# Layer 0's input tiles 0, 1, 6 to 9 by seven products, two modulation blocks behind the query heads, another order at the start, and a folded Fourier product

## The reference

```python
mx = jnp.split((silu_c @ w_mod[l] + b_mod[l])[:, None, :], N_MOD, axis=-1)
mc = jnp.split(silu_cc @ w_mod[l] + b_mod[l], N_MOD, axis=-1)
zx = modulate(rms_norm(x, norm1_g[l]), mx[0], mx[1]) @ w_in[l]
zc = modulate(rms_norm(ctx, norm1_g[l]), mc[0], mc[1]) @ w_in[l]
fx, cqx, ckvx, krx, gx = jnp.split(zx, SPLITS, axis=-1)
...
y = jnp.fft.fftn(u, axes=(1, 3), norm="ortho").real
...
u = a * jax.nn.sigmoid(g)
```

## Time and profile before

| | us |
|---|---|
| median of 3 runs | 1775.14 (1773.23 to 1775.78) |
| the profiled execution | 1775.64 |
| its span | 1772.7 |
| TensorE busy | 1712.4 (97%) |
| VectorE busy | 1013.2 (57%) |
| ScalarE busy | 415.1 (23%) |
| POOL busy | 315.2 (18%) |
| mean transfer rate | 145 GB/s over the span |

### The profile page before, as it was taken

One profiled execution on the slowest core, in us unless ns is written; L12 is line 12 of the kernel. 1 busy time (PEld: TensorE's weight loads), 2 busy tenths in 40 slices (PEclk: granted clock), 3 DMA queues, 4 the chain that ended last, 5 costly groups with the idle time before them and its releaser, 6 DMA issues.

```text
span 1772.7 us, 27384 instructions
## 1 busy us (share of the span) xinstructions
PE 1712.4 (97%) x11010; PEld 1388.0 (78%) x11010; DVE 1013.2 (57%) x1936; ACT 415.1 (23%) x806; POOL 315.2 (18%) x355
## 2 busy tenths in 40 slices
PE   7999999999999999999999999999999999999997
PEld 5434456688888888756799998877888787899997
DVE  1238666756676444496488764277831432288883
ACT  1312463322102110336322110323421101211110
POOL 0000271133001220006144110077000000001110
PEclk9999999999999999999999999999999999999999
DMA  7885324232233252321544555343222443344452
GB/s 274 321 315 197 132 106 170 80 135 95 98 140 115 76 190 91 123 96 34 228 167 167 170 168 187 119 141 129 89 74 86 154 144 118 119 146 164 167 172 91
DMA packets 38744, 256.32 MB, mean 145 GB/s; under 512 B 4161, under 2 KB 7361, under 8 KB 9057
## 3 DMA queue, kind: packets, MB, share of 16 engines
q1 hardware_dynamic: 34544, 228.29, 36.6%
q0 software_dynamic: 3504, 22.15, 3.2%
q10 hardware_dynamic: 576, 4.19, 0.6%
HBM read 247.28 MB, written 7.34 MB: 144 GB/s over the span
## 4 chain that ended last, share of the span: by engine, by line
PE 86%; DVE 8%; ACT 2%; DMA 1%; POOL 1%; issue 1%; ACTq 0%; SPq 0%; DVEq 0%; POOLq 0%
PE ps L707 85%; DMA ring<-weights 1%; POOL aux L2037 1%; PE ps L957 1%; DVE arena L2255 1%; DVE aux L2284 1%; DVE arena L2285 1%; DVE arena L2286 1%; DVE ring L2318 0%; DVE small L2297 0%; DVE aux L2186 0%; DVE aux L2187 0%; DVE aux L2191 0%; DVE aux L2190 0%; DVE aux L2188 0%
## 5 line engine op out<-in xcount | busy, mean ns | idle before, releaser
L707 PE MATMUL ps<-hT,ring 128*128 128x256 f32 (+3 forms) x2976 | 637.1, 374 | 6.8 <-DVE aux L2381 2.1
L707 PEld LDWEIGHTS ps<-hT,ring 128*128 128x128 f32 (+1 forms) x2976 | 505.2, 189 | 125.9 <-issue 64.2
L707 PE MATMUL ps<-arena,ring 128*128 128x256 f32 (+3 forms) x1884 | 355.5, 344 | 4.7 <-DVE arena L2286 3.4
L707 PEld LDWEIGHTS ps<-arena,ring 128*128 128x128 f32 (+1 forms) x1884 | 298.5, 191 | 50.9 <-issue 13.0
L707 PE MATMUL ps<-arena,sums 128*128 128x128 f32 (+1 forms) x966 | 161.6, 317 | 1.3 <-DVE aux L2373 1.3
L707 PEld LDWEIGHTS ps<-arena,sums 128*128 128x128 f32 x966 | 141.7, 191 | 12.3 <-DVE aux L2373 2.5
L2015 POOL TENSOR_TENSOR aux<-aux 128x256 f32<-128x256 f32 (+1 forms) x40 | 41.9, 1047 | 373.3 <-ACT aux L1566 304.4
L2317 DVE TENSOR_TENSOR sums<-ring 128x512 f32<-128x512 f32 x86 | 60.1, 699 | 64.1 <-PE ps L707 59.3
L707 PE MATMUL ps<-hT,sums 128*128 128x128 f32 (+1 forms) x616 | 95.1, 301 | 0.4 <-DVE aux L2373 0.4
L707 PEld LDWEIGHTS ps<-hT,sums 128*128 128x128 f32 x616 | 83.7, 191 | 5.3 <-DVE aux L2373 0.8
L2037 POOL TENSOR_SCALAR aux<-aux,small 128x512 f32<-128x512 f32 (+1 forms) x48 | 71.2, 1492 | 79.5 <-DVE small L2304 78.8
(11 more groups left out here) (384 smaller groups left out, 1980.2 us busy)
## 6 DMA issues: line engine op xcount, KB each, us to landing
ring<-weights SPq DMA_DIRECT2D x212, 1024.0 KB, 4.9
arena<-ahead POOLq DMA_DIRECT2D x8, 1024.0 KB, 9.4
kept_turns<-aux ACTq DMA_DIRECT2D x4, 1024.0 KB, 5.9
arena<-kept_turns POOLq DMA_DIRECT2D x6, 512.0 KB, 4.5
kept_keys_values<-spare POOLq DMA_DIRECT2D x1, 2048.0 KB, 8.4
hT<-ahead POOLq DMA_DIRECT2D x2, 1024.0 KB, 6.1
spare<-ahead POOLq DMA_DIRECT2D x2, 1024.0 KB, 12.3
arena<-kept_keys_values POOLq DMA_DIRECT2D x1, 2048.0 KB, 9.0
```

The source lines that it names most:

```text
L707: ins = nc.tensor.matmul(o_, lhsT, rhs, start=start, stop=stop, skip_group_check=True)
```

## The change

1. The pairs of tiles (6, 7), (8, 9), (0, 1) of layer 0 are computed as quads with seven products. The activations' forms lie where the query heads will be (`qT`). Blocks 4, 5 stand before the first pair, 6, 7 before the second, 8 before the third, 9 behind tile 4, 10 behind the query heads, 11 behind the values. VectorE's sums, forms and combinations are placed by hand; the third pair is combined after ten taps.
2. The turn, the read and the gain that belong to blocks 4 to 11 move into the attention, the turn into step 1, the read and the gain into step 2 (`MOD_BEHIND_TURN, MOD_BEHIND_READ = 1, 2`); the blocks of layer 1 move from steps 2, 5, 8, 11 to 4, 7, 10, 13.
3. The Fourier product over the tokens computes the cosine part for 129 and the sine part for 127 columns of each side; VectorE makes the other half by symmetry (`unfolded`).
4. At the start the memory's tiles are the first transfers of SyncE; ScalarE issues the tables, the vectors and the condition; the table of the root comes first, Silu later; keys 0 and 1 come before block 0; TensorE multiplies zeros five times before the memory's sums and six times behind them.

```diff
@@ constants
-MOD_TURN_STEP = 13
-MOD_READ_STEP = 15
-MOD_STEP = {2: 0, 5: 1, 8: 2, 11: 3}
+MOD_TURN_STEP = 15
+MOD_READ_STEP = 17
+MOD_STEP = {4: 0, 7: 1, 10: 2, 13: 3}
+TAPS_AHEAD = 10
+FOLD = T // 2 + 1
+FOLDED = ((0, FOLD), (1, FOLD - 1))
+STILL = (5, 6)
+Z_PAIRS = ((6, 7), (8, 9), (0, 1))
+MOD_BEHIND = (MOD_BLOCKS - 2, MOD_BLOCKS - 1)
+MOD_BEHIND_TURN, MOD_BEHIND_READ = 1, 2
@@ weight_stream
+    keys(0, 2)
     mod(0, 0)
-    keys(0, 2)
+    keys(2, 4)
     mod(0, 1)
-    keys(2, 6)
+    keys(4, 6)
     mod(0, 2)
...
+        if l == 0:
+            whole()
+            mod(0, 4)
+            mod(0, 5)
+            for p, pair in enumerate(Z_PAIRS):
+                for role in range(4):
+                    for j in range(4):
+                        out.append((("z", 0, 0, p, 0, role, j), "w_in", 0, z_tile(0, pair[role // 2], 2 * j + role % 2)))
+                for q in ((6, 7), (8,), ())[p]:
+                    mod(0, q)
...
+            if l == 0 and n == 4:
+                mod(0, 9)
@@ TensorE
-            pe.wait_ge(S["first_loaded"], 48)
+            def still(count):
+                for _ in range(count):
+                    nc.tensor.matmul(ps[:, 4, 0:T], zeros[:, 0:P], zeros, start=True, stop=True, skip_group_check=True)
+            pe.wait_ge(S["zeros"], 1)
+            still(STILL[0])
+            pe.wait_ge(S["first_loaded"], 16)
...
+            still(STILL[1])
+            mem_keys(0, 2)
             pe.wait_ge(S["silu_c"], 2)
             mod_block(0, 0)
-            mem_keys(0, 2)
+            mem_keys(2, 4)
...
+                def z_seven(p):
+                    n_quad = quad_first[0, 0, "z", p, 0]
+                    for i, (wf_, af) in enumerate(PRODUCTS):
...
+                        for j in range(4):
+                            if wf_ in ROLES:
+                                lhsT = weight(("z", 0, 0, p, 0, ROLES[wf_], j))
+                            else:
+                                lhsT = sums[:, n_quad % 2, SUMS[wf_], j * P:(j + 1) * P]
+                            if i == 2 and j == 0:
+                                pe.wait_ge(S["quad_sums"], n_quad + 1)
+                            mm(bank(key)[:, o:o + T], lhsT, z_act(af, j, p), o == 0 and j == 0, j == 3,
+                               key if (o + T == 512 or i == 6) and j == 3 else None)
+                if l == 0:
+                    mod_block(0, 4)
+                    mod_block(0, 5)
+                    z_seven(0)
+                    mod_block(0, 6)
+                    mod_block(0, 7)
+                    z_seven(1)
+                    mod_block(0, 8)
+                    z_seven(2)
                 for i, n in enumerate(Z_ORDER):
+                    if l == 0 and any(n in pair for pair in Z_PAIRS):
+                        continue
...
-                    if l == 0:
-                        q = MOD_FIRST + i
-                        if q < MOD_BLOCKS:
-                            mod_block(0, q)
-                        if q == MOD_BLOCKS:
-                            mod_turn(0, 1)
                     if n == 4:
+                        if l == 0:
+                            mod_block(0, 9)
                         kr_sum(l)
...
@@ behind the query heads, before the keys' nope part
+                if l == 0:
+                    mod_block(0, MOD_BEHIND[0])
...
@@ fy: cosines to 0:129 of each side, sines to 129:256, 16 products of 129 and 127 columns
-                            for part, tb in ((0, "cn"), (1, "sn")):
+                        for part, tb in ((0, "cn"), (1, "sn")):
+                            first, end = FOLDED[part] if l == 0 else (0, T)
+                            a = sd * T + (FOLD if l == 0 and part == 1 else 0)
+                            for j in range(2):
...
@@ ahead of fy(0)
+                    mod_block(0, MOD_BEHIND[1])
...
@@ in the attention's steps
+                    if l == 0 and j == MOD_BEHIND_TURN:
+                        mod_turn(0, 1)
@@ ScalarE
+            act.dma_start(tab[:, 0:NTAB_FIRST], table_in[:, 0:NTAB_FIRST]).then_inc(S["first_loaded"], 16)
+            act.dma_start(vec[:, :], vectors).then_inc(S["vec_loaded"], 16)
+            act.dma_start(cs_raw[:, :, :], c_in).then_inc(S["c_loaded"], 16)
+            act.wait_ge(S["zeros"], 1)
+            table_of(ACT.Sqrt, zeros[:, 0:1])
...
@@ squares of the memory and the root, and only then
+            did(f(cs[:, :, CS_WIDE - 32:CS_WIDE - 30], cs_raw[:, :, :], ACT.Silu), "silu_c", wait=False)
+            table_of(ACT.Sqrt)
...
+                if l == 0:
+                    for p, pair in enumerate(Z_PAIRS):
+                        first_product(0, "z", 0, p)
+                        taken(act, ("z", 0, 0, p, 3))
+                        for n in pair:
+                            if n >= 8:
+                                did(f(conv[:, n - 8, :], conv[:, n - 8, :], ACT.Sigmoid), "conv_gates")
+                            elif n < 2:
+                                did(f(sq[:, n, 0:2 * T], z[:, n, :], ACT.Square), "lora_squares")
...
@@ fourier_out("fy") becomes cosines_out (columns 0:129 of each side); after the wf copies
+                    mod_rows_out(0, 1)
@@ VectorE
-            dve.wait_ge(S["first_loaded"], 48)
+            did(v.memset(zeros, 0.0), "zeros")
             did(v.memset(cs[:, :, :], 0.0), "silu_c")
+            dve.wait_ge(S["vec_loaded"], 16)
...
+            def z_forms():
+                dve.wait_ge(S["h_ready"], KD)
...
+                did(tt(t1, b12, b11, ALU.subtract), "z_forms")
+                did(tt(t3, b22, b12, ALU.subtract), "z_forms")
+                did(tt(t2, b22, t1, ALU.subtract), "z_forms")
+                did(tt(t4, b21, t2, ALU.subtract), "z_forms")
+                if l == 0:
+                    z_first = quad_first[0, 0, "z", 0, 0]
+                    weight_sums(z_first)
+                    z_forms()
+                    weight_sums(z_first + 1)
+                    combined(0, "z", 0, 0)
+                    weight_sums(z_first + 2)
+                    combined(0, "z", 0, 1)
...
+                        dve.wait_ge(S["conv_gates"], k + 1)
...
-                for tap, k in rest[:TAPS_EARLY[l]]:
+                for i, (tap, k) in enumerate(rest[:TAPS_EARLY[l]]):
+                    if l == 0 and i == TAPS_AHEAD:
+                        combined(0, "z", 0, 2)
                     conv_tap(tap, k)
...
-                mods(l, 1, 4 * MOD_FIRST, N_MOD if l == 0 else 4 * MOD_PARTS[2][1])
-                gains(l, 4 * KD, "norm2_g", 2 * l + 1)
+                if l == 1:
+                    mods(l, 1, 4 * MOD_FIRST, 4 * MOD_PARTS[2][1])
+                    gains(l, 4 * KD, "norm2_g", 2 * l + 1)
...
+                def unfolded(c):
+                    key = ("fy", 0, c)
+                    dve.wait_ge(S["fy_cosines"], c + 1)
...
+                    did(v.tensor_tensor(far, near, sines, ALU.subtract), wait=False)
+                    did(v.tensor_tensor(near, near, sines, ALU.add), key=key)
+                if l == 0:
+                    for c in range(2):
+                        unfolded(c)
...
@@ in the attention's steps
+                    if l == 0 and j == MOD_BEHIND_READ:
+                        mods(0, 1, 4 * MOD_FIRST, N_MOD)
+                        gains(0, 4 * KD, "norm2_g", 1)
@@ SyncE
-            sp.dma_start(tab[:, 0:NTAB_FIRST], table_in[:, 0:NTAB_FIRST]).then_inc(S["first_loaded"], 16)
-            sp.dma_start(cs_raw[:, :, :], c_in).then_inc(S["first_loaded"], 16)
-            sp.dma_start(vec[:, :], vectors).then_inc(S["first_loaded"], 16)
```

More of the change, by code:

```diff
@@ L106, with z_order @@
 WO_PAIRS = 3
+Z_PAIRS = ((6, 7), (8, 9), (0, 1))
+MOD_BEHIND = (MOD_BLOCKS - 2, MOD_BLOCKS - 1)
+MOD_BEHIND_TURN, MOD_BEHIND_READ = 1, 2
+def z_order():
+    return [("z", 0, p, 0, 1) for p in range(len(Z_PAIRS))]
 def wo_order():
@@ L457, in two_blocks @@
         sums = sb("sums", [P, 2, 3, 512])
+        zeros = sums[:, 0, 0, 0:T]
         pend = sb("pend", [P, 4, NCH])
```

204 lines of the change are left out of this document (119 added, 85 removed).

## The result

The changed kernel takes 1794.32 us (median of 4 runs, 1790.22 to 1800.02), the kernel before in the same session 1775.46: ratio 1.011, interval 1.0095 to 1.0125, 19 us slower. Forecast were 1779.5 and a range up to 1784.5. The profiled execution took 1793.09 us, its span is 1791.3, against 1775.64 and 1772.7 before: 18.6 us of span to find.

What follows compares the result with a forecast made beforehand. TensorE was taken as the bound (86% of the chain), VectorE from head 0 of the queries. wf 3.6 us later plus 0.8 in the attention gave 4.4: 1779.5 against 1775.1, own range 1776.5 to 1782, whole range 1769.5 to 1784.5.

Steps and rivals of the forecast that it cites:

- the clock: Rival: TensorE falls to 1.2 GHz after idling before pairs 0 and 1; 2.9 us each, 1782.4 or 1785.3; chance 0.18.
- The waits on the ring: Projection stage: two blocks together outrun the ring; 4.85 us before each of pairs 0 and 1, plus 3.1 for POOL's store.
- the start of the taps, S + 49.7: VectorE's taps begin 49.7 us after the projection stage's start S = 79.0, at 128.7, where before they began at 118.75.
- the sum up to the end of pair 1: Projection stage: pair 1 ends at S + 44.4, from 11.9 (start of pair 0), 12.08, 8.4 and 12.08.
- what VectorE's longer chain delays: After the taps: query vectors ready at 172.8, kr_turned 179.1, last head ends 197.9, values start 4.7 us later.
- The shift carries to the z stage: Start: 3.4 us won at the keys carry through the ring's requests, so the projection stage starts at 79.0, before 82.41.
- The attention: Attention stage: row copy, turn, reads and gain add 0.8 us, bounds 0 and 2.5, later blocks filling some POOL waits.
- the fold: Fourier products before wf: 128 columns instead of 256, 3.5 us less, 0.5 net back in the handover to wf.
- the pair at full clock: Projection stage: a pair with seven products takes 12.08 us on TensorE, against 14.14 for two tiles.
- the keys' start: Start of the kernel: the first key products begin at 12.9, bounds 12.1 to 15.8.
- the time from the values to the end of wf: After the heads: values start at 197.9, block 11 stands in the open for 1.85 us, wf ends at 211.0.
- POOL's copy holding an operation of VectorE with two SBUF inputs: Head 0 of the queries: its third operation is held until POOL's copy ends at 182.8, costing 1.5 us.

Runs made afterwards that it cites:

- kernel 3: Changed kernel with its TensorE waits filled by products of a table whose results are not read: 1788.59 us, ratio 1.0075.
- Kernel 1: Changed kernel with the same work, but one modulation block between any two pairs, blocks 8 and 9 behind tiles 2 and 4: 1776.0 us, ratio 1.0006.
- kernel 5: Changed kernel with POOL's 2 MB store from spare held until pair 2 of the seven products has ended: 1789.82 us, ratio 1.0084.
- Kernel 2: Changed kernel with the rotated keys' bank taken from the two holding banks: 1793.57 us, ratio 1.0101.
- kernel 4: Kernel before with only part 4 of the change (order at the start, products of zeros): 1774.81 us, ratio 0.9995.
- kernel 10: kernel 9 with block 0 ahead of the first keys, Silu ahead of the root, second group of products of zeros gone: 1767.67 us, ratio 0.9956.
- kernel 11: Kernel before with the folded Fourier products and the changed start, block 0 first, without the seven products: 1771.65 us, ratio 0.9979.
- kernel 12: Changed kernel with only attention steps moved: layer 1's blocks in 2, 5, 8, 11, moved turn in 0, its reading in 1: 1797.35 us, ratio 1.012.
- kernel 9: kernel 8 with blocks 10 and 11 behind the query products and their turn behind the keys' products: 1771.14 us, ratio 0.9974.
- kernel 8: Kernel 1 with the edits of Kernel 2 and kernel 5, and blocks 10 and 11, their turn and reading ahead of the values: 1773.39 us, ratio 0.9986.

## Why the prediction was wrong

**The step that failed first** is the clock, which stood in the sum at nothing. The rival was named, its place right (idle twice within 10 us before each of two pairs), and given 0.18 "since the one long idle time was cold and these are shorter". The granted clock is 0.50 from 86.2 to 95 and from 116.1 to 120, and kernel 3 gives 5.7 us back by filling the waits. Its price was nearly right: 2.9 for each fall, by halving 5.7 us of slow work, where each pair lost 3.1 (15.2 for 12.1). With two falls that rival said 1785.3, which the stated range (up to 1784.5) left out; and the measured time is 9 us above even that, for the reasons below. The Trainium skill (TensorE: Matmul & The Clock Gate, Why this matters for your kernels) warns of idle gaps between bursts of matmuls; by that rule alone this case would have been the likeliest, and the trace agrees: 0.50 behind waits of 3.72 + 4.08 and of 3.24 + 1.56 us. The trace of before held evidence on the same side, which the prediction did not read. It uses its longest later wait, 2.1 us, as a sign that it has no long ones; behind that very wait the granted clock is 0.50:

```profile
1082.22 3.23 PE L707 MATMUL ps<-hT,ring 128*32 128x256 f32 x16 [2.12 <-DVE aux L2381]
```

```profile
1082.80:1086.20 3.40, 3.36 (x13) 0.86 (x6) 0.28 (x1) 2.24 (x6) 0.20 (x1) 0.50 1.00 399
```

**The waits on the ring** were right: 7.8 before pair 0 (7.95 forecast: 4.85 and 3.1 for the store), 4.8 before pair 1 (4.85). Kernel 1 takes away all but 1.89 of them, and kernel 5 the store's share alone (3.9). The forecast of the start of the taps, S + 49.7, was missed by 6.3, all of it the clock. The working has two slips that cost nothing: the sum up to the end of pair 1 uses 11.9 and 8.4 where its own terms give 11.65 and 8.55, and 2.5 chunks at 2.45 us need 6.1 of the 8.92 us that they had before, so the ring was not at its limit there.

**A step that was not there.** The list of what VectorE's longer chain delays had the heads and the copy on POOL; it had not the bank. Five banks rotate among z tiles, Fourier tiles and queries. The rotated keys' bank is freed by VectorE at the end of its key work, which stands behind 36 us of taps, and these begin 17 us later than before; so the fourth Fourier tile and everything behind it on TensorE waited until 185.6, and head 0 reached VectorE at 191.65, after the copy that was to hold it. Net 3.9 us. Kernel 2 gives 3.2 of it back in its profiled execution, while its median moved by less than the noise; so the wait is shown, its price in the time is not.

**"The shift carries to the z stage"** held in the profiled execution (79.72 for 79.0) and failed as a rule: with this start alone there was no gain (kernel 4). A shift of TensorE moves the requests only where the order of consumption stays; here the order of block 0 and the first keys changed, and the fifth chunk was requested at 21.5 instead of 17.2. With block 0 first (kernels 10 and 11) the first later request goes out at 13.66 and 13.57, and the stage starts at 80.98 and 80.74, 1.4 and 1.7 earlier than before, half of the 3.4 that the forecast counted; kernel 11's time shows no gain clear of the noise from it.

**The attention** was put at 0.8, with 2.5 as its bound; it was 2.8, beyond the bound: the term was mis-sized by 2.0. The filling by later blocks, for which the forecast took the low value, did not happen at the stage's start: a wait of 1.83 for POOL where the block had been, and behind it another low clock (2.59 for a block of 1.92). How much each part of the 2.8 has was not settled: kernel 12, which moved the steps alone, made it longer.

**Right were**: the fold (3.25 for 3.0), the pair at full clock (12.2 to 12.3 for 12.1), the keys' start (13.3 for 12.9), the time from the values to the end of wf (13.5 for 13.1). POOL's copy holding an operation of VectorE with two SBUF inputs was right as a mechanism: it did not occur in the changed kernel, whose heads came after it, and the operation took 2.79 us for 0.68 where heads met it (kernels 2, 9 and 10). The Trainium skill (GPSIMD Engine Reference, Specifications) names the shared interfaces; the trace agrees.

**Open** stays why equal waits let the clock fall in one execution and not in the next, and how much of the difference between kernels 10 and 11 is the pairs' and how much that of the blocks behind the queries, which were not tried apart.

## What to carry to other kernels

Price a wait of TensorE with what follows it: here each burst of two blocks cost its waits (7.8 and 4.8 us) and about 3 us more of work at half the clock, and spreading the blocks was worth 18 us. Read the granted clock behind every wait that the trace already has, the short ones too. When an engine's chain grows, go through every bank it frees and name the next user, and the same for a moved read of a shared bank. When the order in which a ring is consumed changes, work out the request times again: an earlier start that asks for its fifth chunk later gave nothing here. And before a microsecond or two between two executions is put down to an edit, compare the stages that the edit doesn't touch.

## What the runs showed that was not expected

- Short waits can be enough for the low clock. After waits of 0.38 and 1.47 us 32 records of key products took 8.83 us (kernel 12), after 1.42 and 1.51 as well (kernel 10); after 0.75 and 1.49 they took 7.14 (kernel 9). After 2.46 us eight records took 5.25 (kernel 9), after 2.51 3.70 (kernel 10). After two waits of 1.04 the values' first eight took 3.70 in the kernel before and 5.40 in kernel 4.
- A 2 MB store beside the ring's requests delays them: it landed after 13.1 us (8.4 in the kernel before), and the chunk requested with it after 14.3, against 8.2 without it. It is not the burst of two blocks that does it: in kernel 1, with one block between the pairs, they took 13.0 and 15.1. Why it landed sooner in the kernel before is open.
- Products of zeros at the start worked in most executions (the sums took 3.7 to 3.9 us for 6.46), but in kernel 8 the sums still took 5.82 after five of them (ten records).
